# One mean product instead of two, and statistics moved later, in a two-layer hybrid decoder trunk

## The reference

```python
def conformer_conv_mixer(z, w_conv, b_conv, ln_g, ln_b):
    a, g = jnp.split(z, 2, axis=-1)
    u = a * jax.nn.sigmoid(g)
    u = causal_dwconv(u, w_conv) + b_conv.astype(u.dtype)     # 31 taps, 256 channels
    return jax.nn.silu(layernorm(u, ln_g, ln_b))              # mean, then variance, over the 256 channels
...
    cq, ckv, kr = jnp.split(z, (MLA_Q_RANK, MLA_Q_RANK + MLA_KV_RANK), axis=-1)
    q = (rmsnorm(cq, g_q) @ w_uq)...                          # cq: 384 channels
    kv = (rmsnorm(ckv, g_kv) @ w_ukv)...                      # ckv: 128 channels
```

## Time and profile before

| | us |
|---|---|
| median of 3 runs | 1184.47 (1184.22 to 1184.69) |
| the profiled execution, its own time | 1183.27 |
| its span, first to last instruction | 1181.2 |
| TensorE busy in it | 1163.4 |
| VectorE busy | 809.7 |
| ScalarE busy | 580.7 |
| GpSimd busy | 213.9 |

### The profile page before, as it was taken

The page is one execution under the profiler, slowest core; times in us unless marked ns, Lnnn a source line. Parts: engine busy times, 40 slices in busy tenths (PEclk is TensorE's granted clock), DMA queues, the critical chain, the costliest instruction groups (busy, mean ns, idle before and its releaser), DMA issues.

```text
span 1181.2 us, 15210 instructions
## 1 busy us (share of the span) xinstructions
PE 1163.4 (98%) x5926; PEld 984.9 (83%) x5926; DVE 809.7 (69%) x1081; ACT 580.7 (49%) x879; POOL 213.9 (18%) x203
## 2 busy tenths in 40 slices
PE   7999999999999999999999999999999999999998
PEld 6897888898888888888898887888888888888886
DVE  5799786886666666544759888858766666664464
ACT  4455685643444444334445647855544434443432
POOL 2385282100000000000016734712000000000000
PEclk9999999999999999999999999999999999999999
DMA  8233343533333332566533333345333333336574
GB/s 256 77 90 87 94 135 108 160 103 95 107 90 103 93 101 95 175 193 223 187 99 90 92 85 87 108 148 156 105 91 106 91 90 106 92 105 198 176 223 151
DMA packets 155177, 146.81 MB, mean 124 GB/s; under 512 B 4799, under 2 KB 135779, under 8 KB 155107
## 3 DMA queue, kind: packets, MB, share of 16 engines
q1 hardware_dynamic: 154528, 145.12, 41.1%
q10 hardware_dynamic: 579, 0.74, 0.2%
HBM read 139.54 MB, written 2.10 MB: 120 GB/s over the span
## 4 chain that ended last, share of the span: by engine, by line
PE 89%; DVE 5%; ACT 3%; issue 1%; DMA 1%; POOL 1%; SPq 0%; DVEq 0%; POOLq 0%; ACTq 0%
PE ps L579 28%; PE ps L580 28%; PE ps L581 28%; PE ps L910 1%; PE ps L641 1%; POOL cf_out L1009 1%; PE ps L885 1%; ACT prob L1701 1%; DVE wsp L474 1%; DVE hid L1361 1%; DMA x<-in_x 0%; DVE xn L1134 0%; DVE pv_sum L1342 0%; DVE hid L1255 0%; PE ps L861 0%
## 5 line engine op out<-in xcount | busy, mean ns | idle before, releaser
L579 PE MATMUL ps<-xn,wsp 128*128 128x512 f32 (+1 forms) x1120 | 411.9, 368 | 0.8 <-DVE wsp L474 0.2
L581 PE MATMUL ps<-xn,wsp 128*128 128x512 f32 (+1 forms) x1120 | 408.8, 365 | 0.0
L474 DVE TENSOR_TENSOR wsp<-raw,wsp 128x1024 fp32r<-128x1024 f32 (+2 forms) x249 | 307.0, 1236 | 148.5 <-ACT wsp L466 148.0
L580 PE MATMUL ps<-xn,wsp 128*128 128x512 f32 (+1 forms) x1120 | 408.6, 365 | 0.0
L466 ACT ACTIVATE wsp<-raw 128x1024 fp32r<-128x1024 f32 (+2 forms) x256 | 266.2, 1041 | 166.8 <-PE ps L581 128.9
L579 PEld LDWEIGHTS ps<-xn,wsp 128*128 128x128 f32 x1120 | 211.3, 189 | 36.7 <-DVE xn L1134 2.1
L580 PEld LDWEIGHTS ps<-xn,wsp 128*128 128x128 f32 x1120 | 211.3, 189 | 33.8 <-issue 0.5
L581 PEld LDWEIGHTS ps<-xn,wsp 128*128 128x128 f32 x1120 | 211.2, 189 | 33.6
L579 PE MATMUL ps<-wsp,hid 128*128 128x512 f32 (+1 forms) x488 | 190.4, 390 | 0.6 <-DVE sc_w L1304 0.6
L581 PE MATMUL ps<-wsp,hid 128*128 128x512 f32 (+1 forms) x488 | 189.2, 388 | 0.0
L580 PE MATMUL ps<-wsp,hid 128*128 128x512 f32 (+1 forms) x488 | 189.1, 387 | 0.0
(11 more groups left out here) (161 smaller groups left out, 1184.1 us busy)
## 6 DMA issues: line engine op xcount, KB each, us to landing
raw<-in_w_ffn_up SPq DMA_DIRECT2D x88, 512.0 KB, 3.8
raw<-in_w_ffn_down SPq DMA_DIRECT2D x88, 512.0 KB, 3.8
raw<-in_w_in SPq DMA_DIRECT2D x36, 512.0 KB, 3.9
raw<-in_w_out SPq DMA_DIRECT2D x32, 512.0 KB, 3.7
x<-in_x SPq DMA_DIRECT2D x4, 512.0 KB, 8.1
xn<-xn SPq DMA_DIRECT2D x8, 256.0 KB, 3.2
raw<-in_w_vkr SPq DMA_DIRECT2D x4, 432.0 KB, 3.3
out_x<-x SPq DMA_DIRECT2D x3, 512.0 KB, 5.1
```

The lines of the kernel that those rows point to most:

```text
L474: eng.tensor_tensor(wsp[:, u % SPLIT, 1, 0:nk * n], raw[:, (l * NU + u) % RAW, 0:nk * n], fp(wsp[:, u % SPLIT, 0, 0:nk * n]), ALU.subtract ...
L579: pe.matmul(dst, a[0], b[0], start=start, stop=False, skip_group_check=True)
L580: pe.matmul(dst, a[0], b[1], start=False, stop=False, skip_group_check=True)
L581: return pe.matmul(dst, a[1], b[0], start=False, stop=stop, skip_group_check=True)
```

## The change

The change has three parts, in both layers. GpSimd adds the convolution's two chunks into `cf_tmp[:, 0]` (new line L1016 of the changed kernel, after the `ckv` power and ahead of the sums for `cq`), and TensorE makes the mean with one product of that sum; it stands one `k` step later in group 17. The `cq` statistic moves from after step 2 of group 18 to after step 5. The `ln` statistic, the `cq` spread and the `ln` spread move from group 18 into group 19, behind its steps 0, 3 and 5.

```diff
+        cf_both = sem("cf_both")
...
                         if g == 17:
                             dense(g, bank_of(g), x_pairs, ks=range(1))
                             spread("ckv", l)
+                            dense(g, bank_of(g), x_pairs, ks=range(1, 5))
+                            pe.wait_ge(cf_both, l + 1)
+                            pe.matmul(ps[:, CF_BANK, :], ones[:, :], cf_tmp[:, 0, :], start=True, stop=True)\
+                              .then_inc(mean_done, 1)
+                            last = dense(g, bank_of(g), x_pairs, ks=range(5, KD))
+                        elif g == 18:
+                            dense(g, bank_of(g), x_pairs, ks=range(6))
+                            stat("cq", l)
+                            last = dense(g, bank_of(g), x_pairs, ks=range(6, KD))
+                        elif g == 19:
+                            dense(g, bank_of(g), x_pairs, ks=range(1))
+                            stat("ln", l)
                             dense(g, bank_of(g), x_pairs, ks=range(1, 4))
-                            pe.wait_ge(cf_conv, l + 1)
-                            pe.wait_ge(cf_sum, (l + 1) * (CF_TAPS - 1))
-                            for c in range(2):
-                                last = pe.matmul(ps[:, CF_BANK, :], ones[:, :], cf_out[:, c, :], start=c == 0, stop=c == 1)
-                            last.then_inc(mean_done, 1)
-                            last = dense(g, bank_of(g), x_pairs, ks=range(4, KD))
-                        elif g == 18:
-                            dense(g, bank_of(g), x_pairs, ks=range(3))
-                            stat("cq", l)
-                            dense(g, bank_of(g), x_pairs, ks=range(3, 6))
-                            stat("ln", l)
+                            spread("cq", l)
+                            dense(g, bank_of(g), x_pairs, ks=range(4, 6))
+                            spread("ln", l)
                             last = dense(g, bank_of(g), x_pairs, ks=range(6, KD))
...
-                    if g == 18:
-                        spread("cq", l)
-                        spread("ln", l)
...
                 rsqrt("ckv", l)
+                pool.wait_ge(cf_conv, l + 1)
+                pool.wait_ge(cf_sum, (l + 1) * (CF_TAPS - 1))
+                pool.tensor_tensor(cf_tmp[:, 0, :], cf_out[:, 0, :], cf_out[:, 1, :], ALU.add).then_inc(cf_both, 1)
                 sums("cq", l)
```

## The result

The changed kernel takes 1194.59 us (median of 5 runs, 1193.89 to 1196.22), the kernel before in the same comparison 1184.22 us (1183.79 to 1184.69, 5 runs). The ratio is 1.0091, 95% interval 1.008 to 1.0102: slower by 10.4 us, where the forecast was slower by 3.4 us and the range ended at 1190.2. The profiled execution is the one of 1194.59 us, with a span of 1192.5 us.

A forecast was written before the change was run, and what follows sets the result against it. TensorE, 98% busy, and VectorE's chain behind the spreads were taken to bound the kernel together at group 24. The chain's 1.68 us delay in two layers gave 1184.47 + 3.4 = 1187.8 us, range 1185.8 to 1190.2.

The forecast's parts named there:

- What bounds the kernel, and units: TensorE busy 98%, waiting in group 24 for VectorE's chain, 0.5 us lost; mean product 0.86 us, statistic or spread 0.89 us.
- Step 2, the add: GpSimd's new add ahead of the mean: takes about 1.5 us, hidden, with 0.4 to 1.3 us to spare before 113.15.
- the rule's 113.0: End of GpSimd's new add if it starts only behind VectorE's first weight split, at about 111.7.
- the rows' 112.1: End of GpSimd's new add by the earlier profile alone, starting at 110.56 and taking 1.5 us.
- Steps 3 to 5, the shift: Groups 18 to 24: spreads land later with inputs ready; VectorE's `ln` multiplies and L1304 come 1.68 us later per layer.
- Step 6: TensorE in group 24 stands still about 3.0 us instead of 0.5; the 0.86 us saved only lengthens this wait.
- the first rival, the clock: TensorE returns at half speed behind group 24's gap: 1.87 us more per layer, 1191.5 us; 9 in 100.
- The sum: Whole kernel: +1.68 us per layer, two layers, +3.4 us, giving 1187.8 us, +0.28%.

## Why the prediction was wrong

**What bounds the kernel, and units.** Right. The wait in group 24 is where the change decides, VectorE's chain behind the spreads sets it, and the mean product, the statistics and the spreads cost what was read from the earlier trace rows: the `cq` and `ln` spreads start at 126.14 and 128.42, forecast 126.11 and 128.36.

**Step 2, the add.** Right in what was asked of it: the mean product starts at 113.16 without waiting. The new add takes 2.21 us from 110.64 and ends at 112.85, near the rule's 113.0 and 0.7 us behind the rows' 112.1. It does not start late, at 111.7, as the rule was worked out there: the profile shows an early start and a longer instruction. The two kept splits of VectorE take 3.46 us, as before. What the step did not count is the sum behind it. GpSimd's timeline in the changed kernel:

```profile
110.64 2.21 POOL L1016 TENSOR_TENSOR cf_tmp<-cf_out 128x512 f32<-128x512 f32 x1 [1.34 <-DVE cf_out L1324]
112.81 2.27 POOL L991 TENSOR_TENSOR sq<-sq 128x512 f32<-128x512 f32 x1
115.82 1.49 POOL L991 TENSOR_TENSOR sq<-sq 128x512 f32<-128x512 f32 x1 [0.74 <-ACT sq L1556]
```

The `cq` sums run up to 117.3 and slow VectorE's taps, so that VectorE is 1.3 us late at 119.5. In the full change later waits cover this; with the mean's part alone it cost VectorE's chain 1.0 us in the first layer, and with the fall of the clock 2.4 in the second.

**Steps 3 to 5, the shift.** The start of L1245's counterpart is exact: 129.51. The step that failed is the sentence behind it, that the 10.96 us from L1245 to L1304 hang on nothing that moves. They hang on GpSimd's split of the next unit, which starts when ScalarE's part of it (L467) is done and came earlier (138.43 to 137.80), while VectorE's low parts came later (135.59 to 137.29). The stretch took 142.59 - 129.51 = 13.08 us. The prediction weighed the memory rule at the place of the new add, and not at the place to which the change pushed old instructions. By the Trainium skill's page SBUF — State Buffer, section Who interferes with whom, a VectorE instruction with two SBUF inputs and a GpSimd instruction that reads SBUF contend, and the one that issues second is blocked. The trace agrees: the three low parts took 4.17 - 2.07 = 2.10 us longer when a split of 2.45 us began during the first of them, and in the kernel before, where the split came second, it was the split that took 0.3 us longer.

**Step 6 and the first rival, the clock.** The mechanism was right and priced (1.87 us per gap against 1.57 measured), but it got 9 in 100, with the argument that a gap of 3 us is under half of the one at the start. The gap was 4.9 us by the collision. And the chance seems too low even for 3 us: of the two gaps of 2.84 us in the profile of the run with the split held back, one lowered the clock. Two cases are few, but they fit that run's four times.

**The sum.** Forecast 3.4 us; measured 10.4. By the profiles of before and after the parts are 3.4 (late spreads), 4.2 (collision) and 3.1 (clock). By the medians of the runs they are 4.1 (1187.88 against 1183.82), 3.4 (1191.27 against 1187.88) and 3.3 (1194.59 against 1191.27); the two ways agree within 0.8 us for each part. The direction came out as forecast, and so did the first part; two thirds of the loss come from the two parts that its sum did not have.

## What to carry to other kernels

When a change moves one engine's chain against another's, list what every other engine runs beside the moved instructions, before and after, and not only beside the new ones: a chain's length is its own only as long as its neighbours stay. If TensorE waits somewhere by a few tenths of a microsecond, the chain behind that wait is the bound there, and work taken from TensorE ahead of it only lengthens the wait. A new gap on TensorE of a few microseconds should be priced with the slow restart as part of the forecast, not as a remote case.

## What was not expected of the hardware

The clock falls for less idling than the prediction thought. Behind waits of 4.9 us it was low in all four cases of the two profiles with such gaps (0.50 in whole stretches of 2 us), behind 2.84 us in one of two, and behind 1.43 us together with the narrow products of a statistic in one of two, with the same instructions around it in both layers. It was never low behind the waits of up to 0.7 us of the kernel before. One fall behind group 24's wait cost between 1.3 and 2.4 us (1.57 and 1.54 in the changed kernel, 1.57 with the split held back, 2.4 and 1.3 with the moved pieces alone). Useless products in the gap, 4.3 us of them, made the kernel 3.3 us faster.

The granted clock of a stretch has to be read beside the distance of the products. At the start the four products of the earlier trace rows took 3.75 us, twice what they take later, while the column reads 1.00 in the same stretch of the kernel before:

```profile
8.00:10.00 2.00, 2.00 (x4) 0.55 (x3) 1.35 (x2) 1.07 (x2) 0.46 (x2) 1.00 1.18 318
```
